# Down units of a row moved behind the next row's first gate unit, two waits and one ScalarE step moved near the end

## The chip, the cores and the metric

The kernel runs on one core of a Trainium2 chip. The metric is the device time of one execution in microseconds (us). The engines are named as in the profile: PE is TensorE's matmul stream and PEld its weight loads, DVE is VectorE, ACT is ScalarE, POOL is GpSimd, and SP is SyncE, whose queue issues all of the kernel's DMAs.

## What is computed

One layer of a hybrid encoder on 544 tokens, 512 of a prompt and 32 of running streams. D is 1024, the width of the feed-forward part (D_FF) is 2816, and everything is float32:

```python
def swiglu(x, w_gate, w_up, w_down):
    return (jax.nn.silu(x @ w_gate) * (x @ w_up)) @ w_down
...
        mo, c_new, v_rows = mixer(rmsnorm(x, norm_mix[l]), ...)
        x = x + mo
        x = x + swiglu(rmsnorm(x, norm_ffn[l]), w_gate[l], w_up[l], w_down[l])
    return rmsnorm(x, norm_final), ...
```

The change touches the SwiGLU, its last product and the final norm. The mixer ahead of them stays as it is.

## The kernel before

**Products in three parts.** Each float32 factor is kept as a high part and a low part (`w_hi` and `w_lo`, `xf_hi` and `xf_lo`), both of the type fp32r, and each product is three matmuls: high by high, high by low, low by high (lines 836 to 838 and 639 to 641). ACT makes a high part with a cast, DVE makes the low part by a subtraction.

**Units of seven products.** Where a 1024 x 256 block of weights meets the tokens, the kernel cuts both into 2 x 2 blocks and forms seven products of sums of blocks (`PRODUCTS`) in place of eight. One such piece is a *unit*: 7 products x 4 blocks x 3 matmuls = 84 matmuls of 272 columns. For the unit after the running one, DVE adds blocks of weights (`w_sums`, line 1763 and 1759), ACT casts them into `w_hi` (line 1144) and DVE writes `w_lo` (line 1773). Products 0, 1, 2 and 4 of the running unit go into PSUM banks that are used again at once, so ACT copies them out (`copy_part`, line 1155), and PE waits for the copy: product 6 of a unit waits for the copy of product 4 (`part_copied`). ACT does all of this in one order, in `seven`: behind product 2 it casts weight group 2 of the next unit, for which it waits for DVE's `w_sums`, and behind product 4 it copies product 4.

**The feed-forward part in rows.** The 2816 columns are cut into 11 pairs of 256, in three rows of 4, 4 and 3 pairs (`PAIRS`). A pair is a gate unit and an up unit. The order of units is the table `FFN` (line 82): the gate and up units of row 0, then four *down* units of row 0 which multiply the 1024 columns made by `w_down`, then row 1 likewise, then the 3 pairs of row 2. Below, gate(c,m), up(c,m) and down(c,m) are unit m of row c. The product of row 2 by `w_down` is made in another way, in the last phase (`down`, eight units of 36 or 72 matmuls on 128 output columns each).

When an up unit is done, its result h is split into six sums with high and low parts (`hf_hi`, `hf_lo`, and `s4_hi` and `s4_lo`, named s_hi and s_lo in the profile). ACT does it in `h_second`, `h_first`, `h_sums`, `h_sum2`, `h_sum4`, DVE in `low_second` to `low_sum4`, lines 2084 to 2136. For pairs 0 to 2 of a row this stands among the work of the next gate unit. For pair 3 the next unit is down(c,0), which needs the whole of it. So down(c,0) has a routine of its own: `first_down` on PE (line 870) begins with the blocks of pairs 0 to 2 for products 0, 1 and 5, and takes the last block afterwards, product 5 opens the bank by itself, and product 0 is parked in `parts_first` and added later on DVE (line 2281). On DVE `down(n)` with m == 0 splits h first and only then prepares the weights of down(c,1) (line 2236 on).

**The end.** After the last up unit ACT loads the table of the square root (line 1488) ahead of `split_down`, the cast of the weights for unit 1 of the last phase. DVE waits for `gf_all` (`gf_loaded`), the table of `norm_final`, before its `split_down` for the same weights (line 2287). The DMA of that table is issued when product 6 of the last feed-forward unit is done, since it lands where the tokens' blocks were. The last output block is worked in two parts of tokens (`LAST`): DVE adds the residual (`x_last`, line 2344), ACT squares it (line 1503), PE sums the squares (line 1024), ACT takes the root (line 1505), DVE makes 1/root in four short steps, and the rows of `y_tok` are scaled (ACT line 1509 for two of five chunks, DVE line 2385 for the others) and stored with six DMAs.

Of the kernel before, what the change touches and what calls it, by code (L numbers as in the profile page):

```python
# [26 lines left out]
P = 128  # L27
# [54 lines left out]
FFN = tuple((kind, c, n) for c, pairs in enumerate(PAIRS)  # L82
            for kind, n in [(kind, n) for n in range(pairs) for kind in ("gate", "up")] + [("down", n) for n in range(4 if c < 2 else 0)])
# [50 lines left out]
def trunk_kernel(nc, x_t, cols, w_in, w_quads, ln_g, ln_b, w_s, b_s, w_pa, w_pb, w_o, w_gate, w_up, w_down_quads, w_down, norm_final,  # L134
# [26 lines left out]
    ALONE = [0, QG] + [QG + n for n, (kind, _, m) in enumerate(FFN) if kind == "down" and m == 0]  # L161
# [3 lines left out]
    with ctx:  # L165
# [95 lines left out]
        parts_first, _ = sb("parts_first", [P, HALF], at=tok_at + 24 * N + 12 * HALF)  # L261
# [362 lines left out]
        def _(pe):  # L624
# [202 lines left out]
            def product(q, s, f, blocks, forms, there=None, opening=(0, 1), used=1):  # L827

                _, _, x, bank = PRODUCTS[f]
                out, opens = banks[s][bank], f in opening  # L830
# [8 lines left out]
                if blocks[-1] == KQ - 1 and used:  # L839
                    last.then_inc(form_used, used)  # L840

            def seven(q, s, first=None, behind={}, bank_b=None, forms=x_forms):

                def there(x, k):
                    pe.wait_ge(xf_ready, NPROD * (first + k) + X_ORDER.index(x) + 1)

                for f in range(NPROD):
# [18 lines left out]
                    product(q, s, f, range(KQ), forms, there if first is not None else None)  # L866
                    if f in behind:
                        behind[f]()

            def first_down(q, s, c):  # L870

                made = 5 * (KQ * c + KQ - 1)

                def there(x, k):
                    if k == KQ - 1:
                        pe.wait_ge(hf_ready, made + {A11: 1, A12: 2, A22: 2, S3: 3, S1: 3, S2: 4, S4: 5}[x])

                def part(f, blocks, used=1):
                    product(q, s, f, blocks, h_forms, there, (0, 1, 5), used)

                known, last = range(KQ - 1), (KQ - 1,)
                pe.wait_ge(*first_free(q - 2))
                pe.wait_ge(quad_out, 2 * q - 2)
                pe.wait_ge(hf_ready, made)
                pe.wait_ge(form_lo, NGROUP * q + FORM_AT[1])
                part(0, known)
                part(1, known)
                pe.wait_ge(form_lo, NGROUP * q + FORM_AT[1] + 1)
                part(5, known)
                part(0, last)  # L890
                part(5, last, used=0)
# [1614 lines left out]
```

## Time and profile before

| | |
|---|---|
| median of 3 runs | 856.38 us (855.93 to 857.24) |
| the profiled execution, its own time | 856.78 us |
| its span in the profile | 854.7 us |
| PE busy | 841.1 us, 98% |
| DVE busy | 700.1 us, 82% |
| ACT busy | 448.2 us, 52% |
| POOL busy | 17.4 us, 2% |

The span is the time from the first to the last instruction in the trace. The profiled execution took 2.1 us more than its span, and 0.4 us more than the median. A matmul of 272 columns begins some 0.126 us after the one before while it is shown with a duration of 0.29 us, since matmuls overlap in the array. So stretches of PE are best read by the start times of matmuls.

### The profile page before, as it was taken

What the parts mean: (1) busy time and instruction counts of PE and PEld (TensorE: products, weight loads), DVE (VectorE), ACT (ScalarE), POOL (GpSimd) and SP (SyncE); (2) the same over time, 40 slices, a digit from 0 to 9 for tenths busy, and PEclk for the clock granted to TensorE, in tenths of its full rate; (3) what the DMA queues carried; (4) which work ended last, traced back from release to release, by engine and by line L of the source; (5) the groups of instructions that cost most, each with busy time, mean ns of one, the idle gap of its engine ahead of it and who ended that gap; (6) DMA issues with size and microseconds to landing.
All of it is one profiled execution on the core that took longest, in us unless ns stands there. A gap on an engine that the chain in (4) does not pass through costs nothing.

```text
span 854.7 us, 16297 instructions
## 1 busy us (share of the span) xinstructions
PE 841.1 (98%) x6654; PEld 837.7 (98%) x6654; DVE 700.1 (82%) x1098; ACT 448.2 (52%) x766; POOL 17.4 (2%) x23
## 2 busy tenths in 40 slices
PE   9999999999999999999999999999999999999996
PEld 9999999999999999999999999999999999999996
DVE  6768878789898989845578899999999999888545
ACT  7432225556566565651256776654566655466422
POOL 0000000000000000000000000000000000000031
PEclk9999999999999999999999999999999999999998
DMA  8333314132333232231542122222222222222322
GB/s 300 114 100 102 105 51 151 50 107 99 108 97 110 93 112 98 96 126 50 178 134 90 51 99 100 99 99 99 100 99 100 99 97 101 99 99 69 93 61 105
DMA packets 39496, 88.49 MB, mean 104 GB/s; under 512 B 2177, under 2 KB 28801, under 8 KB 33025
## 3 DMA queue, kind: packets, MB, share of 16 engines
q1 hardware_dynamic: 39424, 87.49, 30.3%
q8 instruction: 52, 0.85, 0.4%
q14 instruction: 20, 0.16, 0.1%
HBM read 85.10 MB, written 2.38 MB: 102 GB/s over the span
## 4 chain that ended last, share of the span: by engine, by line
PE 95%; DVE 2%; ACT 1%; DMA 0%; issue 0%; POOL 0%; DVEq 0%; ACTq 0%; POOLq 0%
PE ps_main L836 13%; PE ps_main L837 12%; PE ps_main L838 12%; PE ps_main L641 10%; PE ps_main L639 10%; PE ps_main L640 10%; PE ps_t L836 7%; PE ps_t L837 7%; PE ps_t L838 7%; PE ps_g L782 1%; PE ps_g L684 1%; DVE w_lo L1773 1%; ACT w_hi L1144 1%; PE ps_t L666 1%; DMA gf_all<-in_norm_final_dram 0%
## 5 line engine op out<-in xcount | busy, mean ns | idle before, releaser
L836 PE MATMUL ps_main<-xf_hi,w_hi 128*128 128x272 f32 x756 | 218.6, 289 | 0.0
L837 PE MATMUL ps_main<-xf_lo,w_hi 128*128 128x272 f32 x756 | 218.5, 289 | 0.0
L838 PE MATMUL ps_main<-xf_hi,w_lo 128*128 128x272 f32 x756 | 218.4, 289 | 0.0
L639 PE MATMUL ps_main<-act_hi,w_hi 128*128 128x272 f32 x692 | 201.1, 291 | 0.9 <-DVE w_lo L2287 0.9
L641 PE MATMUL ps_main<-act_hi,w_lo 128*128 128x272 f32 x692 | 200.0, 289 | 0.0
L640 PE MATMUL ps_main<-act_lo,w_hi 128*128 128x272 f32 x692 | 199.1, 288 | 0.0
L1773 DVE TENSOR_TENSOR w_lo<-w_sums,w_hi 128x1024 fp32r<-128x1024 f32 x150 | 129.6, 865 | 26.4 <-ACT w_hi L1144 25.7
L1144 ACT CAST w_hi<-w_sums 128x1024 fp32r<-128x1024 f32 x150 | 113.9, 760 | 57.4 <-DVE w_sums L1763 35.9
L836 PEld LDWEIGHTS ps_main<-xf_hi,w_hi 128*128 128x128 f32 x756 | 142.4, 188 | 0.0
L838 PEld LDWEIGHTS ps_main<-xf_hi,w_lo 128*128 128x128 f32 x756 | 142.3, 188 | 0.0
L837 PEld LDWEIGHTS ps_main<-xf_lo,w_hi 128*128 128x128 f32 x756 | 142.2, 188 | 0.0
L639 PEld LDWEIGHTS ps_main<-act_hi,w_hi 128*128 128x128 f32 x692 | 130.3, 188 | 1.3 <-issue 1.1
L640 PEld LDWEIGHTS ps_main<-act_lo,w_hi 128*128 128x128 f32 x692 | 130.4, 188 | 0.0
L641 PEld LDWEIGHTS ps_main<-act_hi,w_lo 128*128 128x128 f32 x692 | 130.1, 188 | 0.0
L836 PE MATMUL ps_t<-xf_hi,w_hi 128*128 128x272 f32 x420 | 121.6, 290 | 0.0
L837 PE MATMUL ps_t<-xf_lo,w_hi 128*128 128x272 f32 x420 | 121.4, 289 | 0.0
L838 PE MATMUL ps_t<-xf_hi,w_lo 128*128 128x272 f32 x420 | 121.3, 289 | 0.0
L1773 DVE TENSOR_TENSOR w_lo<-w_raw,w_hi 128x1024 fp32r<-128x1024 f32 (+1 forms) x104 | 95.9, 922 | 5.2 <-ACT w_hi L1144 4.9
L1144 ACT CAST w_hi<-w_raw 128x1024 fp32r<-128x1024 f32 (+1 forms) x104 | 83.9, 807 | 15.1 <-PE ps_t L838 9.7
L836 PEld LDWEIGHTS ps_t<-xf_hi,w_hi 128*128 128x128 f32 x420 | 79.1, 188 | 0.4
L838 PEld LDWEIGHTS ps_t<-xf_hi,w_lo 128*128 128x128 f32 x420 | 79.0, 188 | 0.0
L837 PEld LDWEIGHTS ps_t<-xf_lo,w_hi 128*128 128x128 f32 x420 | 79.0, 188 | 0.0
(281 smaller groups left out, 1288.6 us busy)
## 6 DMA issues: line engine op xcount, KB each, us to landing
w_raw<-in_w_quads_dram SPq DMA_DIRECT2D x20, 1024.0 KB, 4.9
w_raw<-in_w_gate_dram SPq DMA_DIRECT2D x11, 1024.0 KB, 4.9
w_raw<-in_w_up_dram SPq DMA_DIRECT2D x11, 1024.0 KB, 4.9
w_raw<-in_w_down_quads_dram SPq DMA_DIRECT2D x8, 1024.0 KB, 4.9
w_raw<-in_w_in_dram SPq DMA_DIRECT2D x6, 1024.0 KB, 5.1
w_raw<-in_w_pa_dram SPq DMA_DIRECT2D x4, 1024.0 KB, 5.4
w_raw<-in_w_pb_dram SPq DMA_DIRECT2D x4, 1024.0 KB, 5.2
w_raw<-in_w_o_dram SPq DMA_DIRECT2D x4, 1024.0 KB, 6.7
```

The lines of the kernel that those rows point to most:

```text
L639: pe.matmul(out, whi, xhi, start=(opens and k == order[0]), stop=False)
L640: pe.matmul(out, whi, xlo, start=False, stop=False)
L641: last = pe.matmul(out, wlo, xhi, start=False, stop=(closes and k == order[-1]))
L666: last = pe.transpose(dst, src[:, c * P:c * P + ROWS[c]], ident[:, :])
L684: pe.matmul(ps_g[:, 1, 0:P], ones[:, :], ones[:, :], start=True, stop=True)
L782: pe.matmul(ps_g[:, 0, c * P:(c + 1) * P], tok[:, c, group], ws_t[:, g, :], start=True, stop=True)
L836: pe.matmul(out, whi, xhi, start=opens and k == 0, stop=False, skip_group_check=not opens)
L837: pe.matmul(out, whi, xlo, start=False, stop=False, skip_group_check=not opens)
L838: last = pe.matmul(out, wlo, xhi, start=False, stop=k == KQ - 1, skip_group_check=not opens)
L1144: act.copy(f_hi[:, form_group(q, f), :], form_source(q, f, s)).then_inc(third_hi if f == 3 else form_hi, 1)
L1773: dve.tensor_tensor(f_lo[:, group, :], form_source(q, f, s), fbits(f_hi[:, group, :]), ALU.subtract).then_inc(third_lo if f == 3 else form ...
```

## The change

It does five things.

1. `FFN` is made by a function that puts the four down units of row c-1 between gate(c,0) and up(c,0). Gate(c,0) now carries the splitting of pair 3, as any gate unit with m >= 1 carries that of the pair ahead of it.
2. Down(c,0) is an ordinary unit now, `first_down`, `parts_first` and the extra add are gone. PE waits in it for the parts of the last block (`h_there`). The down units stand at odd and even places the other way round than before, so they use the other set of PSUM banks and parts.
3. `up_free`, which makes ACT wait before it overwrites `up_sb` or the parts, is adapted to the new order. The form of weights number 3 of a down unit is no longer made apart from number 5.
4. ACT casts the weights of unit 1 of the last phase before it loads the square root's table, and DVE waits for `gf_all` only before `take_y(0, 0)`, which is the first to read it.
5. In the last two parts ACT squares part 1 before it scales the chunk of part 0.

```diff
-FFN = tuple((kind, c, n) for c, pairs in enumerate(PAIRS)
-            for kind, n in [(kind, n) for n in range(pairs) for kind in ("gate", "up")] + [("down", n) for n in range(4 if c < 2 else 0)])
+def ffn_units():
+    order = []
+    for c, pairs in enumerate(PAIRS):
+        for n in range(pairs):
+            order.append(("gate", c, n))
+            if c and n == 0:
+                order += [("down", c - 1, m) for m in range(4)]
+            order.append(("up", c, n))
+    return tuple(order)
...
+                def h_there(x, k):
+                    if k == KQ - 1:
+                        pe.wait_ge(hf_ready, h_made + {A11: 2, A12: 2, A22: 2, S3: 3, S1: 3, S2: 4, S4: 5}[x])
...
-                elif kind == "down" and m == 1:
+                elif kind == "down" and m == 0 and f == 2:
                     act.wait_ge(hf_ready, 5 * KQ * (c + 1))
-                elif kind == "gate" and m == 0 and c:
+                elif kind == "up" and m == 0 and c:
                     act.wait_ge(parts_taken, KQ * c - 1)
-                elif kind == "up" and m == 0 and c:
+                elif kind == "gate" and m == 1 and c:
                     act.wait_ge(parts_taken, KQ * c)
...
+            split_down(p, 0, 0, NF2)
             act.wait_ge(silu_done, NF)
             act.activation(root[:, 0:1], msq[:, 0:1], ACT.Sqrt).then_inc(root_done, 1)
-            split_down(p, 0, 0, NF2)
...
+            last_squares(0)
+            last_root(0)
+            last_squares(1)
+            last_scale(0)
+            last_root(1)
+            last_scale(1)
...
-                split, plain = m and c < 2, m and c == 2
+                split, plain = n and (c < 2 or m == 0), m and c == 2
...
-            dve.wait_ge(gf_loaded, 16)
             split_down(p, 0, 1, NF2)
             take_x2(0, 0, first=True)
             split_down(p, 0, 0, NF2)
             take_x2(0, 1, first=True)
+            dve.wait_ge(gf_loaded, 16)
             take_y(0, 0)
```

**DVE behind up(0,3).** The names: `w_sums` and `w_lo` belong to the weights of the next unit, `hf_lo` and `s_lo` to the splitting of h. Before, from the last step of up(0,3) through the first part of down(0,0):

```order
660 L2069 TENSOR_TENSOR up_sb<-ps_t,gate_sb 128x544
661 L2084 TENSOR_TENSOR gate_sb<-up_sb 128x544
662 L1773 TENSOR_TENSOR w_lo<-w_raw,w_hi 128x512
663 L2115 TENSOR_TENSOR hf_lo<-up_sb,hf_hi 128x272
664 L2090 SCALAR_TENSOR_TENSOR up_sb<-gate_sb,up_sb 128x272
665 L2108 TENSOR_TENSOR hf_lo<-up_sb,hf_hi 128x2x272
666 L2122 TENSOR_TENSOR hf_lo<-gate_sb,hf_hi 128x2x272
667 L2098 SCALAR_TENSOR_TENSOR up_sb<-up_sb 128x272
668 L2129 TENSOR_TENSOR hf_lo<-up_sb,hf_hi 128x272
669 L2136 TENSOR_TENSOR s_lo_121<-up_sb,s_hi_117 128x272
670 L1773 TENSOR_TENSOR w_lo<-w_sums,w_hi 128x512 x2
671 L1759 TENSOR_TENSOR w_sums<-w_raw 128x1024
```

In the changed kernel the same place is the beginning of gate(1,0):

```order
661 L1762 TENSOR_TENSOR w_lo<-w_sums,w_hi 128x512
662 L2058 TENSOR_TENSOR up_sb<-ps_t,gate_sb 128x544
663 L1748 TENSOR_TENSOR w_sums<-w_raw 128x1024
664 L2073 TENSOR_TENSOR gate_sb<-up_sb 128x544
665 L1762 TENSOR_TENSOR w_lo<-w_raw,w_hi 128x512
666 L2095 TENSOR_TENSOR hf_lo<-up_sb,hf_hi 128x2x272
667 L1752 TENSOR_TENSOR w_sums<-w_sums,w_raw 128x512
668 L2079 SCALAR_TENSOR_TENSOR up_sb<-gate_sb,up_sb 128x272
669 L2102 TENSOR_TENSOR hf_lo<-up_sb,hf_hi 128x272
670 L1752 TENSOR_TENSOR w_sums<-w_sums,w_raw 128x512
671 L2085 SCALAR_TENSOR_TENSOR up_sb<-up_sb 128x272
```

The three sums of the next unit's weights, which stood behind the whole split, now stand among it.

**ACT behind the last up unit.** `w_hi` of 128x768 are the weights of the last phase. Before:

```order
699 L1155 ACTIVATE up_sb<-ps_t 128x272
700 L1343 CAST act_hi<-up_sb 128x544 x2
701 L1488 ACT_TABLE_LOAD
702 L1488 ACTIVATE root<-msq 128x1
703 L1477 CAST w_hi<-w_raw 128x768 x2
```

And in the changed kernel:

```order
699 L1135 ACTIVATE up_sb<-ps_t 128x272
700 L1323 CAST act_hi<-up_sb 128x544 x2
701 L1450 CAST w_hi<-w_raw 128x768
702 L1462 ACT_TABLE_LOAD
703 L1462 ACTIVATE root<-msq 128x1
```

The table load moved behind the cast for unit 1, and still stands ahead of the cast for unit 2.

**ACT in the last two parts.** `y_sq` are the squares, `root` the roots, `y_tok` the rows that are stored. Before:

```order
720 L1503 ACTIVATE y_sq<-x_last 128x256
721 L1505 ACTIVATE root<-msq 128x2
722 L1509 ACTIVATE y_tok<-y_tok,rstd 128x1024
723 L1503 ACTIVATE y_sq<-x_last 128x288
724 L1505 ACTIVATE root<-msq 128x3
725 L1509 ACTIVATE y_tok<-y_tok,rstd 128x1024
```

And in the changed kernel:

```order
721 L1478 ACTIVATE y_sq<-x_last 128x256
722 L1484 ACTIVATE root<-msq 128x2
723 L1478 ACTIVATE y_sq<-x_last 128x288
724 L1491 ACTIVATE y_tok<-y_tok,rstd 128x1024
725 L1484 ACTIVATE root<-msq 128x3
726 L1491 ACTIVATE y_tok<-y_tok,rstd 128x1024
```

The squares of part 1 and the scaling of chunk 1 have changed places, and the root of part 1 stands behind both.

## Rows read from the trace of the kernel before

**Rows 1.** Waits of PE, whole span: total us, times, longest us
```profile
PE ps_main L836 <- ACT parts L1155: 3.1, 2, 1.6
```

**Rows 2.** Timeline of PE: start us, us, instruction [idle before <- releaser]
```profile
564.97 0.29 PE L836 MATMUL ps_main<-hf_hi,w_hi 128*128 128x272 f32 x1
...
576.07 0.39 PE L836 MATMUL ps_main<-hf_hi,w_hi 128*128 128x272 f32 x1 [1.55 <-ACT parts L1155]
...
577.69 0.29 PE L836 MATMUL ps_t<-hf_hi,w_hi 128*128 128x272 f32 x1
...
588.40 0.29 PE L836 MATMUL ps_main<-hf_hi,w_hi 128*128 128x272 f32 x1
...
598.97 0.29 PE L836 MATMUL ps_t<-hf_hi,w_hi 128*128 128x272 f32 x1
```

**Rows 3.** Timeline of PE in the second row of units
```profile
683.69 0.29 PE L836 MATMUL ps_t<-xf_hi,w_hi 128*128 128x272 f32 x1
...
694.47 0.29 PE L836 MATMUL ps_main<-hf_hi,w_hi 128*128 128x272 f32 x1
...
705.57 0.39 PE L836 MATMUL ps_main<-hf_hi,w_hi 128*128 128x272 f32 x1 [1.55 <-ACT parts L1155]
...
707.19 0.29 PE L836 MATMUL ps_t<-hf_hi,w_hi 128*128 128x272 f32 x1
```

**Rows 4.** Timeline of ACT, in up(0,3) and down(0,0)
```profile
560.90 1.05 ACT L1144 CAST w_hi<-w_sums 128x1024 fp32r<-128x1024 f32 x1 [1.35 <-DVE w_sums L1763]
...
574.68 1.05 ACT L1144 CAST w_hi<-w_sums 128x1024 fp32r<-128x1024 f32 x1 [2.72 <-DVE w_sums L1763]
575.63 0.39 ACT L1155 ACTIVATE parts<-ps_main 128x272 f32<-128x272 f32 x1
```

**Rows 5.** Timeline of DVE in up(0,3), down(0,1) and down(0,2)
```profile
555.72 0.44 DVE L2136 TENSOR_TENSOR s_lo<-up_sb,s_hi 128x272 fp32r<-128x272 f32 x1
...
557.21 0.69 DVE L1773 TENSOR_TENSOR w_lo<-w_sums,w_hi 128x512 fp32r<-128x512 f32 x1
...
581.71 0.68 DVE L1773 TENSOR_TENSOR w_lo<-w_sums,w_hi 128x512 fp32r<-128x512 f32 x1
...
591.96 0.69 DVE L1773 TENSOR_TENSOR w_lo<-w_sums,w_hi 128x512 fp32r<-128x512 f32 x1
```

**Rows 6.** Timeline of all engines at the start of the last phase
```profile
804.14 1.28 ACT L1488 ACT_TABLE_LOAD   x1
...
805.55 0.82 ACT L1477 CAST w_hi<-w_raw 128x768 fp32r<-128x768 f32 x1
...
806.85 0.29 PE L641 MATMUL ps_main<-act_hi,w_lo 128*128 128x272 f32 x1
806.92 0.96 DVE L2287 TENSOR_TENSOR w_lo<-w_raw,w_hi 128x768 fp32r<-128x768 f32 x1 [2.04 <-DMA gf_all<-in_norm_final_dram]
...
808.02 0.39 PE L639 MATMUL ps_main<-act_hi,w_hi 128*128 128x272 f32 x1 [0.89 <-DVE w_lo L2287]
```

**Rows 7.** Timelines of DVE, ACT and PE in the last two parts
```profile
845.65 0.45 DVE L2344 TENSOR_TENSOR x_last<-resid,ps_main 128x288 f32<-128x288 f32 x1
...
845.62 1.15 ACT L1509 ACTIVATE y_tok<-y_tok,rstd 128x1024 f32<-128x1024 f32 x1 [0.88 <-DVE rstd L2375]
846.68 0.43 ACT L1503 ACTIVATE y_sq<-x_last 128x288 f32<-128x288 f32 x1
848.20 0.21 ACT L1505 ACTIVATE root<-msq 128x3 f32<-128x3 f32 x1 [1.10 <-DVE msq L2366]
...
847.15 0.76 PE L1024 MATMUL ps_main<-ones,y_sq 128*128 128x1 f32 x6 [0.45 <-ACT y_sq L1503]
```

**Rows 8.** Busy time by stretch (PE, PEld, DVE, ACT, POOL), PEclk, DMA share, GB/s
```profile
847.60:850.30 2.70, 0.31 (x4) 0.21 (x3) 1.94 (x9) 1.20 (x2) 0.00 (x0) 1.00 0.97 388
850.30:850.60 0.30, 0.00 (x0) 0.00 (x0) 0.30 (x1) 0.15 (x1) 0.00 (x0) 0.58 0.03 7
850.60:853.80 3.20, 0.00 (x0) 0.00 (x0) 0.18 (x1) 0.00 (x0) 0.00 (x0) 0.50 1.01 368
```

## What the change will do to the time: the prediction

> **What bounds the kernel now.** PE is busy for 98% of the span, so only three things can move the time: its number of matmuls, the stretches in which it waits, and the end, where it has nothing left to do. The number stays: a down unit has 84 matmuls in either form. So I read PE's waits first, then the starts of matmuls around them, then what ACT and DVE did just before, and last the stores.
>
> Among PE's waits the largest group is for ACT's copies of products into `parts`: two times, 3.1 us in all [rows 1]. One lies in down(0,0) at 576.07 us [rows 2], the other in down(1,0) at 705.57 [rows 3]. The first PE start of a unit to that of the next gives its length. Down(0,2) takes 598.97 - 588.40 = 10.57 us, down(0,0) 577.69 - 564.97 = 12.72 [rows 2], down(1,0) 707.19 - 694.47 = 12.72 [rows 3]. The routine for the first down unit thus costs 2.15 us each time: 1.7 at the wait itself, the rest in short holds too small for the wait view.
>
> Why is ACT late? It began to cast weight group 2 of down(0,1) at 574.68, having stood idle 2.72 us for DVE's sums of weights, and only then copied product 4, at 575.63 [rows 4]. Product 6 of PE needs that copy. In up(0,3) the same cast began at 560.90 [rows 4]. Rows 2 put the start of down(0,0) at 564.97, and up(0,3) is one unit, some 10.6, earlier (554.35). So the cast stands 6.55 into up(0,3) and 9.71 into down(0,0). Product 6 begins after 6/7 of a unit, 9.06, and needs the cast (1.05) and the copy (0.4) behind it: the cast must begin by some 7.6. In down(0,0) it can't, since DVE splits the whole of h before it makes a sum.
>
> **Part 1, the new order.** Gate(c,0) takes the split of pair 3. That is no new kind of unit: it is the list of gate(0,3), instruction for instruction. Down(c,0) follows a gate unit, and DVE's share in it is that of down(0,1), with the scaling of the gate in place of the add to the residual, both on 544 columns. What I have to show is that DVE isn't late in this series. I measure its lag by where its form 6 starts (`w_lo` of 512 columns) after the unit's first matmul. In up(0,3), which stands behind a splitting gate unit, it is 557.21 - 554.35 = 2.86 [rows 5]. In down(0,1) it was 581.71 - 577.69 = 4.02 [rows 2, 5], and from there to the next unit's form 6 DVE took 591.96 - 581.71 = 10.25 [rows 5], with the two residual operations of row 0 in it. Against PE's 10.57 it gains 0.3 per unit. So the new down(0,0) starts with 2.86, the next with 2.5, 2.2, 1.9, and up(1,0) with 1.6. The cast of group 2 falls at 6.55 as in up(0,3), 1.05 before the limit of 7.6. Row 1 has no residual scaling and more room.
>
> The waits that come in have room too. PE's product 3 of down(c,0) needs the last split part, `s_lo`. In up(0,3) DVE wrote the one of gate(0,3) at 555.72, done 1.8 after the unit's start [rows 5], against 4.5 + 1.1 for the fourth block of product 3. ACT waits for the same part before it copies product 2, which is finished at 4.5: queued behind it are group 2's cast and everything else of that unit, but it is met 2.7 earlier. The gate's values wait for their up unit in `gate_sb` during four down units, where nothing else writes it.
>
> I take both units at 10.57: 2 x 2.15 = 4.3 us. Two smaller holds of the same kind go as well: down(0,1) took 588.40 - 577.69 = 10.71, 0.14 over, as DVE was still late from the unit before [rows 2]; up(1,3) took 694.47 - 683.69 = 10.78 [rows 3], 0.2 over, where ACT had form 3 of the first down unit to cast on top. Part 1 gives 4.3 + 0.3 = 4.6. Its bounds are 3.1, the shown waits of rows 1 alone, and 4.65.
>
> **Part 2, the start of the last phase.** DVE stood idle 2.04 us for the table of the final norm and then wrote `w_lo` in 0.96, and PE began the second unit at 808.02, where a step of 0.126 after 806.85 would have had it at 806.98 [rows 6]. That is 1.04 lost, and 0.1 more in the slower first matmul. What is late next, with the wait gone? ACT is free at 804.14, where its table load began; it casts instead (0.82), until 804.96, DVE writes `w_lo` until 805.95, 1.0 ahead of PE. Had only DVE's wait gone, the cast at 805.55 would have ended at 806.37 [rows 6] and `w_lo` at 807.35, still 0.4 late, so both edits are needed. The table load (1.28) and the root move to 804.96 to 806.45 and end before the next cast, which must wait for unit 1's matmuls at 806.98 anyway. Nothing is queued behind the table load that wants to start sooner. The wait for the table of the norm now stands before `take_y(0, 0)`, one unit (5 us) later, when it has long landed. SP's next load of weights goes out 2 us sooner; it is free. I take 1.1, between 0.6 (half of it taken by something unseen) and 1.15.
>
> The Trainium skill (ScalarE: Activation LUTs, "What ACT_TABLE_LOAD costs") puts a change of tables at some 2.66 us with a drain of 1.38 behind the load. The trace shows 1.28 and the root and a cast right after it. By the page the next cast would begin 0.6 later than PE's release, and still 3 us before its weights are wanted: this term would stay.
>
> **Part 3, the tail.** `x_last` of part 1 starts at 845.65, but the squares wait in ACT's order for a scaling of 1.15 us and start at 846.68 [rows 7]. An `x_last` takes 0.45 and a squaring follows some 0.08 later, so they can start at 846.18: 0.50 sooner, and with them the sums at 847.15 [rows 7]. The root behind them was at 848.20 and can be at 847.70. The scaling of chunk 1 now runs from 846.5 to 847.67: just in time not to hold it. So the chain gains 0.50. The stores gain less: the DMA engines are busy at 0.97 and 1.01 on either side of one gap, 850.30 to 850.60, at 0.03 [rows 8]. Only this gap can be closed, 0.3 us. The store of chunk 1 starts 0.5 to 0.9 later, but the engines have the store of chunk 0 to work on until about 849. I take 0.3, from 0 (the later store costs what the earlier ones give) to 0.5.
>
> The Trainium skill (DMA: Bandwidth & Descriptors, "Specifications") gives a ceiling of 435 GB/s to the fabric. By it the queue would run dry for longer, and the whole 0.50 would count: 0.2 us more. The rows show 388 and 368 GB/s with the engines full, and the rows decide.
>
> **The sum.** 4.6 + 1.1 + 0.3 = 6.0 us. The profiled execution took 856.78, with a span of 854.7, so it becomes 850.8 and the span 848.7. Its time is 0.4 above the median of 856.38. The median becomes 850.4.
>
> **Rivals.**
> - *DVE's lag comes back.* Gate(c,0) now splits and four down units follow at once. If DVE entered down(c,0) with the 4.02 of rows 5 and not 2.86, each down unit would hold product 6 for a few tenths, as down(0,1) did with 0.14. For it: DVE was nearly full in gate units. Against: gate(0,3) is the same list and leaves 2.86. Price: up to 2.3 us over both rows, so about 852.7. Chance 0.08.
> - *The last phase gives little.* The weights of its unit 1 are ready, but something of the table's DMA, such as the load queued behind it on SP, then holds a later unit. For it: only one wait of that phase is visible. Against: all other units there stand in even steps of 5 us. Price 1.1, so 851.5. Chance 0.05.
> - *The split's last part comes late, and ACT stands at the copy of product 2 of down(c,0).* Behind it are group 2's cast, product 4's copy and all of PE's later products. It decides once `s_lo` comes later than 4.5 into the unit; it comes at 1.8 in the same place. Were it late by a whole unit's work of DVE (some 8 us past that point in both rows together with the lag it leaves), the cost passes the gain of 6.0 and the kernel is slower: about 858. Chance 0.02.
> - *The tail's gain is all of 0.5, or none*: 850.2 or 850.7, inside the forecast. That the order doesn't change as said can be left out: the order of instructions shows each move.
>
> **How the numbers follow.** The forecast has 0.85: 850.4, with its own range of 849.6 to 851.2 (4.65 + 1.15 + 0.5 at one end, and 4.3 + 0.9 + 0 at the other, give or take 0.2 from run to run). The range reaches to the second rival and part of the first: 849.6 to 852.0. This kernel can be told from no change when it moves by about 0.2%, 1.7 us, so faster means under 854.7. The forecast and the first two rivals all lie there: 0.95. For same I leave 0.03, for slower 0.02.
>
> **What will show it.** Right, if no down unit of the new trace is longer than 10.6 us by PE's starts, if the waits of PE for `parts` and for `w_lo` are gone, if group 2's cast in down(c,0) begins 6.4 to 6.7 into the unit, and if the DMA share has no gap between the stores. Wrong, if product 6 of a down unit still begins more than 9.1 after its first matmul, if PE's second unit of the last phase still starts late, or if the time at the end shrinks by 0.5 or not at all.

## The result and the profile after

The changed kernel takes 851.19 us in the median (851.00 to 851.40), the kernel before, timed beside it, 856.26 (855.93 to 857.24). The ratio is 0.9938, with a 95% interval of 0.9923 to 0.9953: faster by 5.1 us, and by more than 0.2%. The forecast was 850.4, with a range of 849.6 to 852.0. Its sign, size and range held; it was 0.8 too hopeful, and most of what follows is about where these 0.8 are.

The profiled execution took 851.09 us, 5.69 less than the one before, with a span of 849.2. Both traces are level up to the first matmul of gate(0,0), at 476.09 us in each. From there the difference can be laid out by start times of instructions. The last output block is worked in two parts of tokens, 0 and 1, which are not to be confused with parts 1 to 3 of the prediction. "Tail" is the time from the start of `x_last` of the second of them (part 1 of the tokens) to the last instruction.

| stretch | before | after | gain | forecast |
|---|---|---|---|---|
| gate(0,0) to the first unit of the last phase | 326.36 | 321.69 | 4.67 | 4.6 |
| its first unit to its second | 5.57 | 4.52 | 1.05 | 1.1 |
| its second unit to the last `x_last` | 37.63 | 37.54 | 0.09 | 0 |
| tail | 9.08 | 9.32 | -0.24 | 0.3 |
| time around the span | 2.05 | 1.92 | 0.13 | 0 |

The waits of PE (engine, tile and line, releaser: total us, times, longest) hold no `parts` and no `w_lo` any more. These three are all that is left, against [rows 1]:

```profile
PE ps_g L696 <- POOL ident L2384: 1.7, 1, 1.7
PE ps_g L988 <- DVE x_last L2315: 0.5, 1, 0.5
PE ps_g L687 <- ACT r_diag L1330: 0.2, 1, 0.2
```

The timeline of PE (start us, us, instruction) shows the first matmuls of gate(0,0), down(0,0), down(0,1), down(0,2), down(1,0), down(1,1) and of the last phase. The first down units, 12.72 before [rows 2, 3], take 586.10 - 575.53 = 10.57 and 713.11 - 702.54 = 10.57:

```profile
476.09 0.29 PE L848 MATMUL ps_main<-xf_hi,w_hi 128*128 128x272 f32 x1
...
575.53 0.29 PE L848 MATMUL ps_t<-hf_hi,w_hi 128*128 128x272 f32 x1
...
586.10 0.29 PE L848 MATMUL ps_main<-hf_hi,w_hi 128*128 128x272 f32 x1
...
596.67 0.29 PE L848 MATMUL ps_t<-hf_hi,w_hi 128*128 128x272 f32 x1
...
702.54 0.29 PE L848 MATMUL ps_t<-hf_hi,w_hi 128*128 128x272 f32 x1
...
713.11 0.29 PE L848 MATMUL ps_main<-hf_hi,w_hi 128*128 128x272 f32 x1
...
797.78 0.29 PE L651 MATMUL ps_main<-act_hi,w_hi 128*128 128x272 f32 x1
```

ACT's cast of group 2, 9.71 into down(0,0) before [rows 4], now begins 582.24 - 575.53 = 6.71 into it, and 709.43 - 702.54 = 6.89 into down(1,0):

```profile
582.24 1.05 ACT L1124 CAST w_hi<-w_sums 128x1024 fp32r<-128x1024 f32 x1 [1.50 <-DVE w_sums L1752]
583.33 0.40 ACT L1135 ACTIVATE up_sb<-ps_t 128x272 f32<-128x272 f32 x1
...
709.43 1.05 ACT L1124 CAST w_hi<-w_sums 128x1024 fp32r<-128x1024 f32 x1 [1.69 <-DVE w_sums L1752]
```

DVE's form 6 in down(0,0) to down(0,3) and in up(1,0), the measure of its lag [rows 5], stands 3.01, 2.70, 2.38, 2.07 and 1.75 after the unit's first matmul (first and last of the five rows; the last unit began at 617.80):

```profile
578.54 0.69 DVE L1762 TENSOR_TENSOR w_lo<-w_sums,w_hi 128x512 fp32r<-128x512 f32 x1
...
619.55 0.68 DVE L1762 TENSOR_TENSOR w_lo<-w_sums,w_hi 128x512 fp32r<-128x512 f32 x1
```

The start of the last phase, to be held against [rows 6]: the cast comes first, `w_lo` waits for no one, and PE goes on from 802.18 to 802.30 without a hold.

```profile
799.36 0.84 ACT L1450 CAST w_hi<-w_raw 128x768 fp32r<-128x768 f32 x1
800.22 1.28 ACT L1462 ACT_TABLE_LOAD   x1
...
800.23 0.96 DVE L2258 TENSOR_TENSOR w_lo<-w_raw,w_hi 128x768 fp32r<-128x768 f32 x1
...
802.18 0.29 PE L653 MATMUL ps_main<-act_hi,w_lo 128*128 128x272 f32 x1
802.30 0.29 PE L651 MATMUL ps_main<-act_hi,w_hi 128*128 128x272 f32 x1
```

The tail, to be held against [rows 7]. The squares start 0.48 after `x_last` (before: 1.03), the root 2.02 (before: 2.55). So the chain gained 0.53 us, and yet the tail is 0.24 longer.

```profile
839.85 0.45 DVE L2315 TENSOR_TENSOR x_last<-resid,ps_main 128x288 f32<-128x288 f32 x1
...
840.33 0.44 ACT L1478 ACTIVATE y_sq<-x_last 128x288 f32<-128x288 f32 x1 [1.40 <-DVE x_last L2315]
840.68 1.13 ACT L1491 ACTIVATE y_tok<-y_tok,rstd 128x1024 f32<-128x1024 f32 x1
841.87 0.21 ACT L1484 ACTIVATE root<-msq 128x3 f32<-128x3 f32 x1
...
840.83 0.76 PE L1004 MATMUL ps_main<-ones,y_sq 128*128 128x1 f32 x6
```

The busy time by stretch (columns as in [rows 8]) says that the gap between the stores is gone, as forecast: 844.45 to 845.75 holds what was the gap's place, at 1.02. But the stores end differently. The last two rows cut the final 0.8 us of the stores in two, and in the first of them the DMA engines are busy at 0.07 only. One engine of 16 is 0.06. Most engines had finished by 847.6, and one or two were still at work for 0.8 us. At the very end the packets of 4 KB start 7.83, 7.99, 8.15 and 8.30 us after `x_last` and take 0.159 each: one begins when the one before it ends, as they would on a single engine that is left alone.

```profile
844.45:845.75 1.30, 0.00 (x0) 0.00 (x0) 0.00 (x1) 0.00 (x0) 0.00 (x0) 0.50 1.02 377
845.75:847.57 1.82, 0.00 (x0) 0.00 (x0) 0.00 (x0) 0.00 (x0) 0.00 (x0) 0.50 1.05 377
847.57:847.97 0.40, 0.00 (x0) 0.00 (x0) 0.00 (x0) 0.00 (x0) 0.00 (x0) 0.50 0.07 21
847.97:848.37 0.40, 0.00 (x0) 0.00 (x0) 0.00 (x0) 0.00 (x0) 0.00 (x0) 0.50 0.05 20
```

And there is one packet among the stores that isn't a store. The DMA view of 844.8 to 845.3 (queue and kind: packets, MB, share of 16 engines) lists it, 8 KB of instructions on queue 14:

```profile
q1 hardware_dynamic: 103, 0.18, 98.6%
q14 instruction: 1, 0.01, 3.9%
```

In the trace of before the packet of that queue nearest to the end lies at 846.89, before the first packet of a store (847.65). In the changed kernel it lies at 844.81, 4.96 us after `x_last`, in the midst of the stores. This wasn't in the prediction at all.

### The profile page after: what moved, and what is told of

Same layout as the page of the kernel before. It is cut to its first block, busy times and chain, and to the rows that moved or that the text cites. A ratio compares the mean times of both kernels' runs of the same rounds, so it can differ in the third digit from the quotient of the medians.

```text
span 849.2 us, 16289 instructions
## 1 busy us (share of the span) xinstructions
PE 839.2 (99%) x6654; PEld 837.3 (99%) x6654; DVE 698.3 (82%) x1094; ACT 448.3 (53%) x764; POOL 17.7 (2%) x23
## 3 DMA queue, kind: packets, MB, share of 16 engines
HBM read 85.10 MB, written 2.38 MB: 103 GB/s over the span
## 4 chain that ended last, share of the span: by engine, by line
PE 97%; ACT 1%; DVE 1%; issue 0%; POOL 0%; DVEq 0%; POOLq 0%; ACTq 0%
PE ps_main L848 13%; PE ps_main L849 13%; PE ps_main L850 13%; PE ps_main L653 10%; PE ps_main L651 10%; PE ps_main L652 10%; PE ps_t L848 7%; PE ps_t L849 7%; PE ps_t L850 7%; PE ps_g L794 1%; PE ps_g L696 1%; PE ps_t L678 1%; ACT w_hi L1124 0%; PE ps_main L708 0%; PE ps_main L707 0%; PE ps_main L706 0%
## 5 line engine op out<-in xcount | busy, mean ns | idle before, releaser
L1762 DVE TENSOR_TENSOR w_lo<-w_raw,w_hi 128x512 fp32r<-128x512 f32 (+1 forms) x102 | 95.6, 937 | 5.1 <-ACT w_hi L1124 4.9
L1124 ACT CAST w_hi<-w_raw 128x512 fp32r<-128x512 f32 (+1 forms) x102 | 83.5, 819 | 16.9 <-PE ps_t L850 10.8
```

Source lines behind the costliest of these rows:

```text
L1124: act.copy(f_hi[:, form_group(q, f), :], form_source(q, f, s)).then_inc(third_hi if f == 3 else form_hi, 1)
L1762: dve.tensor_tensor(f_lo[:, group, :], form_source(q, f, s), fbits(f_hi[:, group, :]), ALU.subtract).then_inc(third_lo if f == 3 else form ...
```

## The experiments

A run's time moves by some tenths from execution to execution, in part because the first matmul into `ps_main` starts anywhere from 6.61 to 7.68 us into the span in these 14 profiled executions. So a term of 0.3 us is read from the stretches of the profiled executions, and the times stand beside it. All kernels in one table, in the order in which they are told of:

| kernel | median us (runs) | ratio, 95% interval | gate(0,0) to last phase | unit 1 to 2 | tail | q14 packet after `x_last` |
|---|---|---|---|---|---|---|
| before | 856.26 (4) | | 326.36 | 5.57 | 9.08 | 1.24 |
| changed | 851.19 (4) | 0.9938, 0.9923 to 0.9953 | 321.69 | 4.52 | 9.32 | 4.96 |
| e1_order | 851.87 (4) | 0.9945, 0.9929 to 0.9962 | 321.69 | 5.12 | 9.27 | 4.74 |
| e2_phase | 855.09 (10) | 0.9988, 0.9978 to 0.9997 | 326.34 | 4.52 | 9.09 | 1.24 |
| e3_tail | 856.03 (10) | 0.9997, 0.9988 to 1.0007 | 326.35 | 5.12 | 8.74 | 1.23 |
| e4_oldtail | 850.58 (4) | 0.9929, 0.9913 to 0.9946 | 321.70 | 4.52 | 9.68 | 4.75 |
| e5_gf_only | 850.94 (1) | | 321.70 | 5.05 | 9.32 | 4.96 |
| e7_lag4 | 852.08 (1) | | 324.07 | 4.52 | 8.74 | 1.25 |
| e6_lag2 | 851.13 (1) | | 322.20 | 4.52 | 8.78 | 1.38 |
| e8_pad4 | 850.07 (5) | 0.9925, 0.9911 to 0.9938 | 321.69 | 4.52 | 8.73 | 1.39 |
| e9_order_pad4 | 851.62 (4) | 0.9947, 0.9932 to 0.9962 | 321.71 | 5.12 | 9.07 | 1.67 |
| e11_oldtail_pad4 | 850.63 (4) | 0.9935, 0.9919 to 0.9952 | 321.71 | 4.52 | 9.07 | 1.39 |
| e12_act4 | 851.12 (4) | 0.9942, 0.9925 to 0.9959 | 321.70 | 4.52 | 9.33 | 4.97 |
| e10_halves_pad4 | 850.31 (5) | 0.993, 0.9916 to 0.9943 | 321.68 | 4.52 | 8.69 | 1.68 |

### One part at a time: e1, e2, e3, e4

e1_order is the changed kernel with parts 2 and 3 undone:

```diff
+            act.wait_ge(silu_done, NF)
+            act.activation(root[:, 0:1], msq[:, 0:1], ACT.Sqrt).then_inc(root_done, 1)
             split_down(p, 0, 0, NF2)
-            act.wait_ge(silu_done, NF)
-            act.activation(root[:, 0:1], msq[:, 0:1], ACT.Sqrt).then_inc(root_done, 1)
...
+            dve.wait_ge(gf_loaded, 16)
             split_down(p, 0, 1, NF2)
...
             last_root(0)
-            last_squares(1)
             last_scale(0)
+            last_squares(1)
```

> The new order of units alone; the start of the last phase and the last two parts as in the kernel before. Theory A (the three edits add up, and the order brings 4.7 us, the tail nothing): PE's first down unit of each row takes 10.6 us, x_last of part 1 starts 4.7 us sooner than before, near 841.0, the waits of PE show 0.9 for w_lo of line 2287's kind and none for parts, and the time is 4.7 below the kernel before. Rival (the order alone brings less because something later, for instance the table's DMA, holds the end in place): x_last starts less than 4.4 sooner.

The order of the units alone gives the whole of part 1, 326.36 - 321.69 = 4.67. It also has a tail 0.19 longer than before's, though not one line of the tail differs from before's.

e2_phase is the kernel before with only the cast and the wait for the table of the norm moved (the first two pieces of that diff, the other way round):

> The kernel before with the second edit alone: ACT casts the last phase's weights ahead of the table load, DVE waits for the norm's table later. Theory A: x_last of part 1 starts 1.1 us sooner, the wait of 0.9 is gone, the two waits for parts of 1.55 stay, time 1.1 lower. Rival (the load of weights that follows on SP's queue becomes the next thing that holds a unit): less than 0.9, with a new wait in one of the later units.

It gives 1.05 from the first unit of the last phase to the second and some 0.1 behind it, and its median is 1.1 below that of the 19 runs of before made beside it (856.15). The tail is before's, 9.09.

e3_tail is the kernel before with only the new order of ACT's last instructions (the last piece):

> The kernel before with the third edit alone: the last squares ahead of the scaling. From the start of x_last of part 1 to the end of the span it was 9.08 us in the kernel before and 9.32 in the changed one. Theory A (the stores run one behind the other without a gap and the 16 DMA engines finish unevenly, so the gain of the chain is lost): the root of part 1 comes 0.5 sooner, yet the stretch is 9.2 to 9.4. Rival (the uneven finish was an accident of one trace, and the closed gap is worth its 0.3): 8.7 to 8.9.

Here the tail is 8.74, 0.34 less than before's 9.08, as the prediction had it, and the theory with which the run was made, that this gain would be lost, was wrong. The interval of its ratio takes in no change, so only the trace bears the gain out.

e4_oldtail is the changed kernel with the old order of those instructions, so that the last piece can be judged in the other surroundings:

```diff
             last_root(0)
-            last_squares(1)
             last_scale(0)
+            last_squares(1)
```

> The changed kernel with the order of the last squares and the scaling put back. Theory A: x_last starts near 839.85 as in the changed kernel, and the stretch from it to the end is again 9.0 to 9.1, so the span is 0.2 shorter than with the edit, about 848.9. Rival (accident of one trace): the stretch is 9.3 or spread at random, and over the runs this kernel is 0.3 slower than the changed one.

Its tail is 9.68 against 9.32: the edit is worth 0.36 here too, within 0.02 of e3. But both tails are some 0.6 longer than the same instructions gave in the old order of units (9.68 to 9.08, 9.32 to 8.74). So something that comes with the new order of units, and not the edit, lengthens the end. Neither of the two tails named ahead of the run, 9.0 to 9.1 or 9.3, was met. And the times say the opposite of the traces: without the edit of part 3 the runs took 850.39 to 850.89 us, with it 851.00 to 851.40.

### Which of part 2's edits: e5

The changed kernel with the cast back behind the table load; only the wait for the final table stays moved.

```diff
-            split_down(p, 0, 0, NF2)
             act.wait_ge(silu_done, NF)
             act.activation(root[:, 0:1], msq[:, 0:1], ACT.Sqrt).then_inc(root_done, 1)
+            split_down(p, 0, 0, NF2)
             split_down(p, 0, 1, NF2)
```

> The changed kernel, with ScalarE's cast of the last phase's first unit put back behind the square root and its table load; only the wait for the final weights stays moved. In the execution of the changed kernel TensorE's second unit of that phase began 4.52 us after the first; with neither edit (the order alone) it was 5.12. Theory, the two edits remove two waits that stand one behind the other: w_lo is now made after the table load and the cast, some 1.3 us of table load later, and TensorE waits for it, 0.3 to 0.5 us, so first to second unit 4.8 to 5.0 us. Rival, the wait for the weights was the only one that ended late: 4.5 us as in the changed kernel. Rival two, the weights' wait never mattered in these executions: 5.1 us as with the order alone. Rest as in the changed kernel; time 851.2 to 851.9 us.

PE's second unit comes 5.05 after the first, a little over the 4.8 to 5.0 expected: 0.53 of the gain hangs on the cast, and the prediction's "0.4 late" is what the trace has:

```profile
800.12 0.82 ACT L1450 CAST w_hi<-w_raw 128x768 fp32r<-128x768 f32 x1
...
800.97 0.96 DVE L2258 TENSOR_TENSOR w_lo<-w_raw,w_hi 128x768 fp32r<-128x768 f32 x1 [1.51 <-ACT w_hi L1450]
...
802.07 0.38 PE L651 MATMUL ps_main<-act_hi,w_hi 128*128 128x272 f32 x1 [0.36 <-DVE w_lo L2258]
```

The other half is not a fixed price. In e1, with the wait for the table still in its old place, DVE wrote `w_lo` at 801.86, 0.1 after the cast's end (800.94 + 0.82), and the two units stand 5.12 apart; so do those of e3 and e9. In these executions the table had landed by about the time the cast was done: it took 3.6 or 3.7 us from its issue. In the execution of before it took 4.3 and landed 0.55 after the cast. So moving DVE's wait was worth 0.45 to 0.5 there and 0.07 here.

```profile
800.94 0.82 ACT L1450 CAST w_hi<-w_raw 128x768 fp32r<-128x768 f32 x1
...
801.86 0.96 DVE L2258 TENSOR_TENSOR w_lo<-w_raw,w_hi 128x768 fp32r<-128x768 f32 x1 [1.58 <-ACT w_hi L1450]
```

No run has the cast moved alone. An estimate from the changed kernel: the table was issued at 797.97 and took 3.9, so it landed at 801.9. A `w_lo` of 0.96 begun then would have ended at 802.8, 0.5 after the 802.30 at which PE began the second unit. So once the cast is moved, DVE's wait has to move too.

### How much lag part 1 has room for: e7 and e6

e7_lag4 is the changed kernel with four additions that nothing reads on DVE in each first down unit, ahead of the sums, into a spare tile; e6_lag2 has two of them.

```diff
                 form(q, s, 6)
                 last_of(n)
+                if m == 0:
+                    for _ in range(4):
+                        link(dve.tensor_tensor(spare_row[:], r_all[:, 0:HALF], r_all[:, HALF:N], ALU.add))
```

> The changed kernel with four operations of 128x272 on DVE in down(c,0), each waited for, ahead of the sums of weights of the next unit: they compute nothing that is used. They hold DVE back by 1.7 to 1.9 us in each row. Prediction's rule (the cast of weight group 2 may begin 7.6 us into the unit, it begins at 6.55 now): the cast comes at 8.3, product 6 waits 0.6 to 0.8, down(c,0) takes 11.2 to 11.5 instead of 10.57, the following down units 10.57 or at most 0.1 more. Rival (there is more room than the rule gives, since the wait in the kernel before was mostly for the late sums and not for ACT's order): no unit longer than 10.6.

The four take 1.86, the casts begin 583.33 - 574.72 = 8.61 and 711.68 - 702.78 = 8.90 into their units, and the units are 11.61 and 11.91 long: 1.04 and 1.34 over 10.57. The wait on `parts` is back under its new tile:

```profile
PE ps_t L849 <- ACT up_sb L1136: 1.9, 2, 1.1
...
578.98 1.86 DVE L2232 TENSOR_TENSOR spare_row<-r_all 128x272 f32<-128x272 f32 x4
...
583.33 1.05 ACT L1125 CAST w_hi<-w_sums 128x1024 fp32r<-128x1024 f32 x1 [3.41 <-DVE w_sums L1753]
...
711.68 1.05 ACT L1125 CAST w_hi<-w_sums 128x1024 fp32r<-128x1024 f32 x1 [3.70 <-DVE w_sums L1753]
```

8.61 - 1.04 = 7.57 and 8.90 - 1.34 = 7.56: the prediction's limit of 7.6 is met to a few hundredths. The units are longer than the 11.2 to 11.5 expected, mostly since the expectation counted the lag from a cast at 6.55, and in the changed kernel the casts begin at 6.71 and 6.89. e6 asks whether there is free room ahead of it:

> The changed kernel, with two additions of 128x272 that nothing reads on VectorE in each first down unit (four of them took 1.9 us, so these take some 0.93), ahead of the sums. With four, the casts began 8.61 and 8.90 us into the two units and these were 1.04 and 1.34 us long over the others. Theory, a unit is held by what the cast is late over about 7.6 us: casts at 7.65 and 7.85, holds of 0.1 and 0.3 us, so units of 10.65 and 10.85 us and a stretch from the first matmul of this part to the last phase of 322.0 to 322.2 us (321.69 in the changed kernel, 324.07 with four). Rival, a lag is paid in proportion, with no room ahead of it: half of what four cost, 322.9 us.

With two additions the casts begin 583.31 - 575.64 = 7.67 and 710.71 - 702.76 = 7.95 into the units, which are 10.67 and 10.96 long: holds of 0.10 and 0.39, again the cast less 7.57. A lag paid in proportion would have given 322.9 for the stretch; it was 322.20, 0.51 over the changed kernel.

```profile
583.31 1.05 ACT L1125 CAST w_hi<-w_sums 128x1024 fp32r<-128x1024 f32 x1 [2.46 <-DVE w_sums L1753]
...
710.71 1.05 ACT L1125 CAST w_hi<-w_sums 128x1024 fp32r<-128x1024 f32 x1 [2.75 <-DVE w_sums L1753]
```

### The tail: e8, e9, e11 and e12

What follows was tried on a guess drawn from e1 and e4: queue 14 brings DVE's instructions, 8 KB at a time. DVE now runs 1094 instructions, before 1098, so its last fetch comes later in the program, and there it meets the stores. The test is to give DVE four small instructions more, in the last phase, and change nothing else:

```diff
             take_x2(1, 0)
             take_y(0, 1)
+            for _ in range(4):
+                link(dve.tensor_scalar(msq_rest[:], msq[:], EPS, None, ALU.mult))
             with dve.Fori(1, 3) as j:
```

e8_pad4 is the changed kernel with this, e9_order_pad4 is e1 with it.

> The changed kernel with four small repeated operations (msq_rest of 128x5, each with its wait) on DVE in the last phase, far off the path; they compute nothing new. In every trace with the new order of units an instruction packet of 8192 bytes (queue q14) falls among the last stores, 3.5 to 4.1 us before the end, where in the kernel before, and with the second or third edit alone, it falls 6.7 to 7.0 us before the end, ahead of them. Theory P (DVE's stream became shorter, so that its fetch of instructions slid 3.6 us towards the end and holds up one DMA engine's stores): the packet is back at 1.2 us after x_last of part 1, no late last packets, x_last to end 8.7 to 8.8, where it was 9.32, and the span near 848.6. Rival (the uneven finish belongs to the continuous stores or to chance, and the packet with it): the packet moves and the stretch stays 9.1 to 9.6, or it doesn't move since it is another engine's.

> The new order alone, with the same four small operations on DVE; the start of the last phase and the last two parts as in the kernel before. Theory P: x_last to end 9.1 as in the kernel before (9.08), where the new order alone had 9.27, and the packet at 1.2 us after x_last. Rival: 9.2 to 9.7 as in the other kernels with the new order.

In e8 the packet is back at 1.39 after `x_last`, and the tail is 8.73, that of e3. In e9 it is 9.07, that of before. The end of e8 by the same stretches as above (its first row is the one that ends 1.6 us before the last instruction):

```profile
846.08:847.30 1.22, 0.00 (x0) 0.00 (x0) 0.00 (x0) 0.00 (x0) 0.00 (x0) 0.50 1.06 416
847.30:847.70 0.40, 0.00 (x0) 0.00 (x0) 0.00 (x0) 0.00 (x0) 0.00 (x0) 0.50 0.96 277
847.70:848.10 0.40, 0.00 (x0) 0.00 (x0) 0.00 (x0) 0.00 (x0) 0.00 (x0) 0.50 0.54 154
```

The engines now stop together, 0.96 and then 0.54, where the changed kernel had 0.07 and 0.05. e11_oldtail_pad4 is e4 with the four, and e12_act4 is the control: four instructions more on ACT in place of DVE.

```diff
                 seven(n, beside(n))
+                if n == 22:
+                    for i in range(4):
+                        act.activation(spare_row[:, 8 * i:8 * i + 8], r_all[:, 8 * i:8 * i + 8], ACT.Copy)
```

> The changed kernel with the old order of ScalarE's last instructions (scaling ahead of the second square), and with four VectorE instructions of 128x5 in the last phase that nothing reads. Theory, the store tail is lengthened by the fetch of VectorE's instructions falling among the last stores, and by nothing else of the new order: with the four instructions the fetch comes at about 1.4 us after x_last of part 1, as before the change, and the tail from x_last to the end is 9.1 us (before: 9.08; the same kernel without the four: 9.68), some 0.35 us more than with the new order and the four (8.73). Rival, the 0.6 us came from something else in the new order of ScalarE's last instructions, and the old one keeps 9.6 to 9.7 us whatever VectorE's program holds. Time 850.2 to 850.7 us.

> The changed kernel with four small copies of 128x8 on ScalarE that nothing reads, behind one gate unit in the middle. Theory, the packet of instructions that falls among the last stores belongs to VectorE's program, so four more instructions on ScalarE leave it where it is in the changed kernel (some 5 us after x_last of part 1), with a tail of 9.2 to 9.4 us and 851.0 to 851.5 us. Rival, it belongs to ScalarE's program, or to anything that makes the program longer: the packet goes back to 1 to 2 us after x_last and the tail to 8.7 us, 850.1 to 850.6 us, as with the four on VectorE.

e11 has a tail of 9.07, before's to 0.01, and 0.34 over e8's: with the packet out of the way the edit of part 3 is worth the same for the third time. In e12 the packet stays at 4.97 and the tail at 9.33. So a longer program of ACT doesn't move the packet, a longer one of DVE does. The other kernels fit this: with 1094 instructions on DVE (changed, e1, e4, e5, e12) the packet lies 4.74 to 4.97 after `x_last`, with 1098 to 1102 (before, e2, e3, e6, e7, e8, e9, e10, e11) 1.24 to 1.68. In e6 and e7 the added instructions stand in the down units, far from the end, and the tails are 8.78 and 8.74, so it isn't the place of the four in the last phase that shortens it. The end of e4, of e11 and of e12, the two rows that answer to the last two of e8:

```profile
847.40:847.80 0.40, 0.00 (x0) 0.00 (x0) 0.00 (x0) 0.00 (x0) 0.00 (x0) 0.50 0.11 21
847.80:848.20 0.40, 0.00 (x0) 0.00 (x0) 0.00 (x0) 0.00 (x0) 0.00 (x0) 0.50 0.05 20
```

```profile
847.52:847.92 0.40, 0.00 (x0) 0.00 (x0) 0.00 (x0) 0.00 (x0) 0.00 (x0) 0.50 0.97 277
847.92:848.32 0.40, 0.00 (x0) 0.00 (x0) 0.00 (x0) 0.00 (x0) 0.00 (x0) 0.50 0.53 154
```

```profile
847.11:847.51 0.40, 0.00 (x0) 0.00 (x0) 0.00 (x0) 0.00 (x0) 0.00 (x0) 0.50 0.11 31
847.51:847.91 0.40, 0.00 (x0) 0.00 (x0) 0.00 (x0) 0.00 (x0) 0.00 (x0) 0.50 0.05 20
```

Two things stay open. The trace doesn't say which engine carried a packet, so that the late finisher is the one that fetched the instructions is an inference from the order of the last packets; and the fetch itself takes only 0.3 to 0.4 us, while the tails differ by 0.20 (e1 to e9), 0.59 (changed to e8) and 0.61 (e4 to e11). Nor do the medians follow the tails one by one: they differ by 0.25, 1.12 and -0.05 us for these three pairs. Their mean, 0.44, is near that of the tails, 0.47, but the pair e4 and e11 shows that in executions other than the profiled one the price may be another. The price of the fetch is thus shown in the profiled executions alone.

### Can the first store start sooner: e10

e8 with chunk 0 scaled and stored in two halves (the piece below is DVE's; SP's store of the chunk is cut in two likewise), to see whether the stores' start or their work sets the end.

```diff
-            for cols in (slice(0, D // 2), slice(D // 2, D)) if c == 2 else (slice(0, D),):
+            for cols in (slice(0, D // 2), slice(D // 2, D)) if c in (0, 2) else (slice(0, D),):
```

> As e8_pad4, and chunk 0 of the output is scaled and stored in two halves, as chunk 2 is. With the stores' engines full without a gap, the end hangs on when the first store starts and on how much is stored. Theory S (the stores bound the tail): the first packet comes 0.3 to 0.4 us sooner after x_last (2.0 before), and x_last to end shrinks by about as much against e8_pad4, to 8.4. Rival (the chain of sums and roots bounds it, and one more DMA issue of 0.4 us on SP's queue is in its way): 8.7 to 9.1.

The first packet of a store moves at 1.74 us after `x_last` in place of 2.00, but the last one ends at 7.91 in place of 7.92, and the medians are 850.31 and 850.07. The end of e10, from 5.9 us after `x_last` on:

```profile
845.29:846.48 1.19, 0.00 (x0) 0.00 (x0) 0.00 (x0) 0.00 (x0) 0.00 (x0) 0.50 1.04 401
846.48:846.88 0.40, 0.00 (x0) 0.00 (x0) 0.00 (x0) 0.00 (x0) 0.00 (x0) 0.50 1.14 307
846.88:847.28 0.40, 0.00 (x0) 0.00 (x0) 0.00 (x0) 0.00 (x0) 0.00 (x0) 0.50 0.13 41
```

The head start was real, since the last 0.4 us hold 41 GB/s where e8 had 154. It was given back there: two engines or so finished after the others. No packet of instructions lies among the later stores, but one runs from 1.68 to 1.99 after `x_last`, and with the first store at 1.74 it now overlaps the start of the stores, which it doesn't in e8 (1.39 to 1.86, first store at 2.00). Whether this took back the head start, or the way in which the stores are shared out among the engines, isn't shown. No version has a lower median than e8's 850.07, 6.3 us below before; e10 isn't told from it.

## Why the prediction was right, and where it was off

**What bounds the kernel** was read rightly. All that moved lies in the three places named: PE's matmuls are the same 6654 before and after.

**Part 1 (4.6; measured 4.67).** The step that carried it was to take gate(0,3) and down(0,1) as models of the new gate(1,0) and down(0,0), and to ask only when group 2's cast would begin. Forecast 6.55, measured 6.71 and 6.89, both just outside the 6.4 to 6.7 that was to be a sign of being right. The limit of 7.6 was taken from PE's seventh product, and e7 and e6 put it at 7.57. The slope of DVE's lag was forecast at 0.3 a unit from two rows, and it is 0.31. Two statements were a little off. The lag began at 3.01, not 2.86. And "row 1 has no residual scaling and more room" is wrong for its first down unit: the cast there is 0.18 later than in row 0, so the room is 0.7, not 1.05. Neither cost anything. The small holds went too: down(0,1) is 10.57 and up(1,3) 10.59. None of the eight down units is longer than 10.57.

**Part 2 (1.1; measured 1.05 and 0.09 behind it).** Right, and right in that both edits are needed, for the cast by e5 and for the wait by the estimate there. What it took for granted is that the table of the norm lands as late in each execution as in the one profiled. It doesn't: of the 14 profiled executions it took 4.3 and 4.4 us to land in two (before and e2) and 3.4 to 3.9 in the others. Where it lands in time, the whole part is worth 0.6 (e1 with 5.12 to 4.52), the low end of the term. The times show no such loss: the three pairs that differ by part 2 alone, before to e2, e1 to e4 and e9 to e11, are 1.06, 1.29 and 0.99 apart in their medians. On the table load the trace decides: in the changed kernel the load at 800.22 took 1.28 again, and the root followed at 801.51. The Trainium skill (ScalarE: Activation LUTs, "What ACT_TABLE_LOAD costs") has 2.66 us with the drain. The trace agrees with it on the load alone; no such drain is to be seen here.

**Part 3 (0.3; measured -0.24).** This is the step that failed, and one of the prediction's own signs of being wrong, an end that shrinks by 0.5 or not at all, came true. Its mechanism held: the chain gained 0.53 (0.50 forecast), the gap of the DMA engines closed, and in the traces the edit alone is worth 0.34, 0.36 and 0.34 by e3, e4 and e11. The times don't bear even this out: with the edit the medians are 0.12 lower (before to e3), 0.61 higher (e4 to changed) and 0.56 lower (e11 to e8), so what it is worth over many executions isn't shown. What was missed is that part 1 would touch the tail. By taking four instructions out of DVE's program it moved a fetch of 8 KB from 1.24 to 4.96 us after `x_last`, among the stores, and with it went 0.59 us between the profiled executions of the changed kernel and of e8. The prediction went through DVE's and ACT's order, SP's queue and the stores, but not through the queues of instructions, which the page of the profile lists with their packets.

**The sum.** 0.54 of the shortfall is the tail. The other terms and the time around the span are 0.2 better than forecast, so that the profiled execution gained 5.69 of 6.0. The remaining 0.5 is in the base: the forecast took the profiled execution of before to be 0.4 above its median, and that of the changed kernel was 0.1 below its own. Two executions can differ by more than that in where their first matmul into `ps_main` starts. But the late table of part 2, worth 0.45 in the profiled execution of before, is of the same size, and it may have been counted twice, as gain and as the distance to the median. Which it was isn't shown, since the executions that make the median have no trace.

**The range.** That the time lies well inside 849.6 to 852.0 is luck in part, since the upper end was set by rivals that didn't come true; in the narrower range of 849.6 to 851.2 it lies by 0.01. That range doesn't follow from its own terms. The gains of 6.3 and 5.2 lead to 850.1 and 851.2, and 0.2 either way to 849.9 and 851.4. And they used 4.3 and 0.9 as the low ends of parts 1 and 2, which had been given as 3.1 and 0.6.

**The rivals.** None came true. The lag didn't come back (measured 3.01, not 4.02), and e7 shows what it would have looked like: down units of 11.6 and 11.9. The last phase gave all it could. The late split didn't occur: `s_lo` was written at 577.06, 1.53 into down(0,0), done by about 2. That the time lies beyond the tail's "all of 0.5, or none" is due to a mechanism that was no rival at all.

## What to carry over

Where a wait is let go by an engine that works through a fixed list, look for the place where the same list already stands in another unit: the start times there gave the gain of the two moved units to 0.1 us, and the instant by which the late instruction must begin tells how much lag is free and from where each 0.1 us costs 0.1. Before giving a tail of stores a gain of some tenths, find the packets of instructions near it and ask whether the change shifts that engine's count of instructions. And a term read from a single wait on a DMA is only worth what that DMA's lateness is in the next execution.

## What the hardware showed

An instruction fetch of 8 KB among the last stores went with 0.20 to 0.61 us more in the tail, and the busy share shows its form: 0.05 to 0.11 of the DMA engines at work in the last 0.4 to 0.8 us of the stores, in place of 0.43 to 0.56 in the last 0.4 us of the kernels before, e3, e6, e8, e9 and e11. (In e10 it is 0.13, with no such packet among the last stores.) The price is that of single profiled executions. Four small instructions more on DVE moved it away (e8), and so did the two additions in each of two units (e6). The eight table loads of ACT took 1.28 us each in the changed kernel, and behind six of them the next instruction began 0.01 us later (behind the others 0.3 and 7.8). A small table that a wait hung on landed 3.4 to 4.4 us after its issue, by execution. In the stretches of 1.2 us and more just before the last 0.8 us of the stores, with all engines busy, they ran at 369 to 416 GB/s.
